# Five buffers instead of three for gathered rows of the first table, and a gather slot behind every four scatters instead of every eight

## The reference, cut to what matters

```python
def peer_block(xb, w_pq, sub_keys, u_tab, v_tab):
    q = (xb @ w_pq).reshape(T, PEER_HEADS, 2, D_HALF)
    s = jnp.einsum('thcd,ckd->thck', q, sub_keys)
    ...                                    # top 16 of 16x16 candidates per head
    g = jax.nn.softmax(best, axis=-1)      # 8 heads x 16 experts = 128 per token
    u = jnp.take(u_tab, eidx, axis=0)      # rows of the first table
    a = jax.nn.gelu(jnp.einsum('thkd,td->thk', u, xb))
    vv = jnp.take(v_tab, eidx, axis=0)     # rows of the second table
    return jnp.einsum('thk,thkd->td', g * a, vv)
```

## Time and profile before

| | |
|---|---|
| median of 3 runs | 2699.69 us |
| the profiled execution | 2700.05 us, its span 2698.4 us |
| TensorE busy | 2442.0 us (90%) |
| VectorE busy | 1920.3 us (71%) |
| ScalarE busy | 931.3 us (35%) |
| GpSimd busy | 1175.7 us (44%), 684 instructions |
| GpSimd, scatters L493 | 256 of 1933 ns mean |
| U stage, lo of step 2 to the last matmul | 901 to 1914 us |
| V stage | 1914 to 2698 us |

### The profile page before, as it was taken

The page is one execution under the profiler, slowest core; times in us unless marked ns, Lnnn a source line. Parts: engine busy times, 40 slices in busy tenths (PEclk is TensorE's granted clock), DMA queues, the critical chain, the costliest instruction groups (busy, mean ns, idle before and its releaser), DMA issues.

```text
span 2698.4 us, 37865 instructions
## 1 busy us (share of the span) xinstructions
PE 2442.0 (90%) x13838; PEld 2180.1 (81%) x13838; DVE 1920.3 (71%) x2105; ACT 931.3 (35%) x1018; POOL 1175.7 (44%) x684
## 2 busy tenths in 40 slices
PE   5988889889799999999979988899999989998999
PEld 4867768668699999999978878899877777787777
DVE  4554544543546998989867676777587888888888
ACT  4353543522322333323323222223333333333333
POOL 1020100120000001068788888883576676767662
PEclk9999999989899999999999998899999999999999
DMA  5453443467264668789989999998899999999997
GB/s 196 125 172 109 149 134 110 158 247 286 68 133 109 168 167 228 204 213 217 209 222 249 236 237 231 226 238 222 297 395 378 396 407 392 394 407 385 394 400 298
DMA packets 271975, 661.38 MB, mean 245 GB/s; under 512 B 64953, under 2 KB 114937, under 8 KB 229720
## 3 DMA queue, kind: packets, MB, share of 16 engines
q1 hardware_dynamic: 150736, 334.56, 39.2%
q0 software_dynamic: 82064, 249.26, 27.5%
q10 hardware_dynamic: 39095, 76.57, 11.2%
HBM read 613.65 MB, written 46.02 MB: 244 GB/s over the span
## 4 chain that ended last, share of the span: by engine, by line
PE 31%; POOL 26%; DMA 19%; DVE 12%; issue 8%; ACT 2%; DVEq 1%; SPq 0%; ACTq 0%; POOLq 0%
POOL g_dense L493 17%; PE banks L1291 9%; PE banks L1292 9%; PE banks L1293 9%; POOL a_values L535 6%; DVE h L1243 4%; DMA g_dense<-route,route_place 3%; DMA a_tile<-a_dense 3%; DMA v_row<-in_v_tab,route_place 3%; DMA raw<-in_v_tab 3%; DMA k_cache<-in_cache_k 2%; DMA v_raw<-in_v_tab 2%; POOL u_row L487 2%; DVE u_turned L1120 2%; POOL v_row L526 1%
## 5 line engine op out<-in xcount | busy, mean ns | idle before, releaser
L1291 PE MATMUL banks<-xT_hi,ring_hi 128*128 128x320 f32 (+1 forms) x2304 | 736.6, 320 | 92.8 <-DVE ring_lo L1124 85.5
L1292 PE MATMUL banks<-xT_lo,ring_hi 128*128 128x320 f32 (+1 forms) x2304 | 730.3, 317 | 0.0
L1293 PE MATMUL banks<-xT_hi,ring_lo 128*128 128x320 f32 (+1 forms) x2304 | 729.5, 317 | 0.0
L493 POOL DMA_INDIRECT g_dense<-route,route_place x256 | 494.9, 1933 | 140.8 <-issue 74.1
L1291 PEld LDWEIGHTS banks<-xT_hi,ring_hi 128*128 128x128 f32 x2304 | 443.5, 193 | 104.1 <-issue 92.8
L1292 PEld LDWEIGHTS banks<-xT_lo,ring_hi 128*128 128x128 f32 x2304 | 444.0, 193 | 0.0
L1293 PEld LDWEIGHTS banks<-xT_hi,ring_lo 128*128 128x128 f32 x2304 | 443.1, 192 | 0.0
L526 POOL DMA_INDIRECT v_row<-in_v_tab,route_place x128 | 279.6, 2185 | 182.7 <-DVE h L1243 159.2
L861 DVE TENSOR_TENSOR ring_lo<-raw,ring_hi 128x2048 fp32r<-128x2048 f32 x72 | 164.6, 2291 | 264.8 <-ACT ring_hi L573 264.5
L1120 DVE STREAM_TRANSPOSE u_turned<-raw 128x2048 f32<-128x2048 f32 x128 | 295.6, 2310 | 71.6 <-DMA raw<-in_u_tab 61.6
L1243 DVE SCALAR_TENSOR_TENSOR h<-v_row,w_values,h 128x2048 f32<-128x2048 f32 x128 | 300.4, 2347 | 42.7 <-DMA v_row<-in_v_tab,route_place 39.8
(11 more groups left out here) (219 smaller groups left out, 3869.5 us busy)
## 6 DMA issues: line engine op xcount, KB each, us to landing
raw<-in_u_tab SPq DMA_DIRECT2D x256, 256.0 KB
raw<-in_u_tab ACTq DMA_DIRECT2D x256, 256.0 KB
v_raw<-in_v_tab SPq DMA_DIRECT2D x64, 1024.0 KB
raw<-in_v_tab SPq DMA_DIRECT2D x64, 1024.0 KB
raw<-in_w_in SPq DMA_DIRECT2D x160, 256.0 KB
a_dense<-gelu_out SPq DMA_DIRECT2D x128, 160.0 KB
raw<-in_w_out SPq DMA_DIRECT2D x64, 256.0 KB
g_dense<-zeros POOLq DMA_DIRECT2D x16, 1024.0 KB, 26.2
```

The costliest lines, as they stand in the source:

```text
L493: pool.indirect_dma_start(out=places, out_offset=bass.IndirectOffsetOnAxis(ap=routeU[:, t, 2, j:j + 1], axis=0), in_=route[:, t, 0, j:j + ...
L1291: MM(out, h1, h2, start=first, stop=False)
L1292: MM(out, h1, l2, start=False, stop=False)
L1293: return MM(out, l1, h2, start=False, stop=last)
```

## The change

Three things. From dot 12 on the gathers take turns over five buffers, numbered from (i - 12) % 5; the two new ones lie at WK + 32 and WK + 40, on the routing scratch, so the first gather into each waits for `rt_ready` 3. SyncE's loads into `v_raw0` and `v_raw1`, at the same addresses, now wait for the last dot instead of the routing. And GpSimd's loop has 64 pieces of four scatters instead of 32 of eight; behind each piece come the gathers that are due by the assumed step plus three (before step 56) or five.

```diff
-NUB = 3
+NUB, EARLY = 5, 12
+def u_buffer(i):
+    return i % 3 if i < EARLY else (i - EARLY) % NUB
+def last_in(i):
+    return max((k for k in range(i) if u_buffer(k) == u_buffer(i)), default=-1)
+def uses(i):
+    return sum(u_buffer(k) == u_buffer(i) for k in range(i + 1))
...
-        urow = [at(f"u_row{i}", MX + 8 * i, [P, D]) for i in range(NUB)]
+        urow = [at(f"u_row{i}", kb, [P, D]) for i, kb in enumerate((MX, MX + 8, MX + 16, WK + 32, WK + 40))]
...
-            sp.wait_ge(rt_ready, NT)
+            sp.wait_ge(dot_done, DOTS)
             v_weights(0, 0)
             v_weights(1, 1)
-            sp.wait_ge(dot_done, DOTS)
...
-                if i >= NUB:
-                    pool.wait_ge(dot_done, i - NUB + 1)
+                if last_in(i) >= 0:
+                    pool.wait_ge(dot_done, last_in(i) + 1)
+                elif i >= EARLY:
+                    pool.wait_ge(rt_ready, NT)
...
-            while gathered < dots_after(MIXED - 2 * N_PARTS) + NUB:
+            while gathered < dots_after(MIXED - 2 * N_PARTS) + 3:
                 gather_dot(gathered)
                 gathered += 1
-            for n in range(TD // P * PH * 2):
-                t, h, half = n // (2 * PH), n // 2 % PH, n % 2
-                if n % (2 * PH) == 0:
+            for n in range(TD // P * PH * 4):
+                t, h, part = n // (4 * PH), n // 4 % PH, n % 4
+                if n % (4 * PH) == 0:
                     pool.wait_ge(rt_ready, t + 2)
-                if half == 0 and n:
-                    pool.wait_ge(g_scat, 16 * (n // 2 * TOPK))
-                for k in range(half * TOPK // 2, (half + 1) * TOPK // 2):
+                if part == 0 and n:
+                    pool.wait_ge(g_scat, 16 * (n // 4 * TOPK))
+                for k in range(part * 4, part * 4 + 4):
                     scatter(t, h * TOPK + k)
-                while gathered < min(DOTS, dots_after(38 + (n + 1) * 5 // 2) + NUB):
+                step = 38 + (n + 1) * 5 // 4
+                while gathered < min(DOTS, dots_after(step) + (3 if step < MIXED else NUB)):
                     gather_dot(gathered)
                     gathered += 1
```

More of the change, by code:

```diff
@@ L483, in gather_dot @@
             def gather_dot(i):
-                if i >= NUB:
-                    pool.wait_ge(dot_done, i - NUB + 1)
+                if last_in(i) >= 0:
+                    pool.wait_ge(dot_done, last_in(i) + 1)
+                elif i >= EARLY:
+                    pool.wait_ge(rt_ready, NT)
                 pool.indirect_dma_start(
-                    out=urow[i % NUB][:, :], out_offset=None, in_=I["u_tab"][0],
-                    in_offset=bass.IndirectOffsetOnAxis(ap=uidx[:, i:i + 1], axis=0)).then_inc(urow_in[i % NUB], 16)
+                    out=urow[u_buffer(i)][:, :], out_offset=None, in_=I["u_tab"][0],
+                    in_offset=bass.IndirectOffsetOnAxis(ap=uidx[:, i:i + 1], axis=0)).then_inc(urow_in[u_buffer(i)], 16)
             def scatter(t, j):
@@ L1192, in dot @@
                     dve.wait_ge(xrow_in, 16)
-                dve.wait_ge(urow_in[i % NUB], 16 * (i // NUB + 1))
-                row = urow[i % NUB]
+                dve.wait_ge(urow_in[u_buffer(i)], 16 * uses(i))
+                row = urow[u_buffer(i)]
                 V.tensor_tensor_reduce(row[:, :], row[:, :], xrow[:, :], 1.0, 0.0, ALU.mult, ALU.add, adot[:, i:i + 1]).then_inc(dot_done, 1)
```

## The result

| | before | after |
|---|---|---|
| median, us (20 runs each, lowest to highest) | 2707.3 (2691.57 to 2716.85) | 2715.81 (2701.35 to 2733.0) |
| ratio of the times, compared chip by chip | | 1.0053 [1.0034, 1.0071] |
| profiled execution, us | 2700.05 | 2713.6 |
| its span, us | 2698.4 | 2712.0 |
| GpSimd, mean of the 256 scatters | 1933 ns | 1987 ns |

By the ratio the changed kernel is slower by 0.5%: 0.0053 x 2700 = 14 us, between 9 and 19. The two medians alone lie 8.5 us apart. The forecast was 7.5 us slower, 2707.5, in a range of 2682 to 2726. Two executions of a later run (half of the dot: 2759.69 and 3317.42 us) had a granted clock of 0.87 and 0.78 where all others have 0.96 to 0.97, and are left out of every comparison.

A forecast was written before the change was run, and what follows sets the result against it. GpSimd's own stream was taken as the bound: 11 us at the start, 3.5 and 21.0 for unhidden gathers, less the credit of eight scatters, put dot 63 7.5 us later: 2700.05 + 7.5 = 2707.5 us, range 2682 to 2726.

The forecast's parts named there:

- What bounds the kernel: U stage, 1335 to 1850 us: GpSimd's scatters and gathers make 517 of 515 us; it never waits for VectorE.
- The start: First scatters: gather 10 waits 8.7 us for dot 7 with four scatters behind it; 17th scatter 11 us late.
- Gathers no longer hidden: Scatters 64 to 248: twelve more gathers outside boundaries at 1.754 us, 21.0 us; two before scatter 64, 3.5 us.
- The scatters' duration: Scatters in the stretch up to the last one: held at 1.915 us each, with no added cost in the sum.
- rival A: Singly issued gathers are held by VectorE's two-input instructions: +40 us, 2740, or +24 with half of both; chance 0.10.
- The boundaries: Waits between heads for scatters to land: stay at 5.5 us, up to 2.4 more for each of five with one gather.
- The credit and the last dot: Gather 63 behind 248 scatters instead of 256, at 1861.9 against 1849.35; dot 63 8.8 us later, at 1870.7, +7.5.
- What costs nothing: Behind the last dot: new `v_raw` wait already met, scatters out at 1881.4 before the first `g_tile`, gelu wait some 20 us.
- B: VectorE uses the lead of two more dots, fewer disturbed table loads: about -3 to -25 us; chance 0.22.
- C: Transfers bound the stretch at DMA share 0.97, so the end stays: 2700, at most 15 us won; chance 0.15.
- D: The wait really is gone: all 71.4 us that TensorE lost to late lo's come back, 2629; chance 0.03.

The follow-up runs named there:

- half of the dot: The changed kernel with every dot over the first 1024 of 2048 columns, gathers unchanged: 2679.93 and 2681.11 us, about 0.991 against the kernel before.
- second pair: The unchanged and the changed kernel each profiled once more for a second trace: 2706.46 us before, 2718.79 us after.
- half rows: The changed kernel with dots over 1024 columns and gathers bringing 1024 floats of a row instead of 2048: 2672.74 us, 0.9882 against the kernel before.

## Why the prediction was right, and what it got wrong

**What bounds the kernel: right.** GpSimd's stream does. Halving the scatters took 49 us off, halving the gathered bytes took nothing off before the last dot. The reading that settled it before any run was the releaser in the earlier trace rows: no wait of GpSimd for a dot, so no lack of buffers.

**The start: right in kind, 2 to 5 us too much.** Gather 10 waited 6.99 us for dot 7 (8.7 worked out), and the 17th scatter came 51.8 us behind the first, against 45.8 before: 6 us late, not 11. The second pair has 53.2 against 44.3, 9 us. Up to the 65th scatter the two pairs of traces show +4.1 and +17.6 us, on average 11, where 14.5 had been worked out. A single trace is no measure of this term.

**Gathers no longer hidden: right.** Between scatters 64 and 248, 27 gathers outside a boundary took 45.1 us in the changed kernel, 15 took 26.4 us before: +18.7 us, where 12 x 1.754 = 21.0 had been expected. In the second pair it is 45.8 against 22.7, +23.0. Three buffers with pieces of four, 1.0% slower, show this term without the lead that the buffers bring: 27 such gathers took 43.4 us there.

**The scatters' duration: this term failed.** It was held at 1.915 us and cost nothing in the sum. In the same stretch 184 scatters took 2.008 us each with the idle left out, against 1.910: +18.0 us. In the second pair it is 2.015 against 1.972, +7.9 us, so on average 13 us. It is rival A's mechanism, put at the wrong instruction: I had let it lengthen the 14 new single gathers (their mean stayed, 1443 ns against 1454), and it was the scatters: their excess under a lo is 55.9 and 61.2 us, against 44.1 and 51.5, and under a dot 31.3 and 24.8, against 23.2 and 24.6. That VectorE's two-input instructions make them long is shown, by the half dot and by the scatters above. Why they lose more to them in the changed order is not: one may argue that a stream broken more often falls out of step with VectorE's, but no run here tests it. The buffers alone don't do it: with five buffers and pieces of eight the 184 scatters took 357.1 and 355.7 us, in the kernel before 351.4 and 362.8. Three buffers with pieces of four took 361.1, the changed kernel 369.5 and 370.7.

**The boundaries: no dearer, where zero to +12 was allowed.** Eleven of them took 55.7 us, against 60.6: -4.9. But in the second pair they took 56.0 against 55.5, so the 4.9 are no effect of the change. Those with one gather took 2.6 to 2.9 us four times and 7.8 once, in the second trace 3.9 to 6.1: less than the 5.5 held for them in most cases, in spite of the 7.9 us of the first boundary, which was no guide. Perhaps the scatters land sooner when fewer gathered rows share the DMA engines with them; that was not tried.

Together, scatters, gathers and boundaries: 18.0 + 18.7 - 4.9 = 31.8 of the 31.9 us (522.7 - 490.8), and 7.9 + 23.0 + 0.5 = 31.4 of the 31.5 of the second pair. The sum had 21.0 there. The whole repeats far better than its parts.

**The credit and the last dot: right.** Gather 63 stood 0.3 us behind scatter 248, eight scatters earlier than before, and came 13.0 us later than before (12.5 worked out); dot 63, 6.7 us (7.5). From the gather to the dot it was 7.5 us, and 7.8 in the second trace, between the 8.8 of the sum and the estimate of 4.4 beside it. That the two numbers meet so well is partly luck: 10 us less at the start stand against 11 more behind it. In the second pair of traces dot 63 is 18.6 us later, and +14 us, the measured difference, lies between the two. Over both pairs dot 63 came 12.7 us later on average, 5 more than worked out: 13 us of longer scatters, less 4 at the start, 2 at the boundaries and 2 between gather and dot.

**What costs nothing: right.** The last scatter ended at 1888.5, where 1881.4 had been worked out. The first loads into `v_raw` were issued 24 us behind the last dot and the first `g_tile` 22 us behind the last scatter's end, and GpSimd still had 15.48 us to wait for gelu of the dots. SyncE's queue in the kernel after:

```profile
1897.26 0.86 SPq L390 DMA_DIRECT2D v_raw<-in_v_tab  x2
...
1911.00 0.43 SPq L394 DMA_DIRECT2D g_tile<-g_dense  x1
```

**The rivals.** A, slower by 27 to 40 us, happened at part of its price. B, the lead counts, is true of the buffers alone (0.2 to 0.5% faster), and not with the finer pieces that came with them. C, the transfers, is what stands next: each version with the last dot earlier than before and whole dots has VectorE wait 52 to 93 us for loads, against 41 before. D fell, as GpSimd's missing wait said.

## What to carry to other kernels

Before giving a late transfer more buffers, look at what its issuer waits for: if it never waits for a buffer to come free, more of them cannot make the stream shorter, and little can be gained (here 6 to 12 us of 71, with the order left as it was). Put instructions that only issue work where the engine has to sit out a wait anyway, and count how many leave such a place when an order is made finer. An indirect DMA that GpSimd issued cost more under VectorE instructions with two operands in SBUF (2.1 to 2.8 us against 1.56), so its cost is a matter of both engines' order, and is worth two traces, not one.

## What was not expected of the hardware

- The issue of a scatter on GpSimd took 1.55 to 1.62 us when it began under a VectorE transpose or an idle VectorE, in 1271 of 1280 cases in the twelve traces. Where it began under a lo or a dot, it ended 1.42 to 1.55 us behind that one's end, in 927 of 928 cases. The nine exceptions of the first kind took 3.6 to 3.7 us; each began in the last 0.07 us of a transpose.
- Halving the dot's length (2.29 to 1.22 us) cut the excess of the scatters under a dot from 31.3 and 24.8 us to 5.2, and to 7.5 in the run with half rows. From the 65th scatter to the end of scatter 248 GpSimd took 495.2 and 492.8 us, instead of 522.7 and 525.0.
- Two traces of one and the same kernel differed by 46 ns in the mean of 192 scatters, 9 us, while its times lie within 1% and the stretch around 184 of them differed by 2.7 us: gathers and boundaries took less where the scatters took more.
